# A four-layer hybrid diffusion step on one core: inputs requested at once, squares summed per token tile, layer norm in quarter slots with two forms of k-tile

## What is computed

```python
def rms_norm(x, g, eps=NORM_EPS):
    y = x * lax.rsqrt(jnp.mean(x * x, axis=-1, keepdims=True) + eps)
    return y * g
mod = jax.nn.silu(cond) @ w_mod[i] + b_mod[i]          # w_mod[i]: 1024 x 3072
shift, scale, gate = jnp.split(mod, 3, axis=-1)        # one set for context, one for latent tokens
h = rms_norm(x, norm_g[i]) * (1 + scale) + shift
x = x + gate * mixer(h @ w_in ...)
```

## Time and profile before

| | us |
|---|---|
| median of 3 runs | 2298.48 (2291.75 to 2299.92) |
| the profiled execution | 2295.94 |
| its span | 2294.1 |
| PE busy in the span | 2077.8 (91%) |
| DVE, ACT, POOL busy | 1179.2, 822.3, 550.6 |
| mean granted PE clock | 0.939 of full speed |

### The profile page before, as it was taken

One profiled execution on the slowest core, in us unless ns is written; L12 is line 12 of the kernel. 1 busy time (PEld: TensorE's weight loads), 2 busy tenths in 40 slices (PEclk: granted clock), 3 DMA queues, 4 the chain that ended last, 5 costly groups with the idle time before them and its releaser, 6 DMA issues.

```text
span 2294.1 us, 35050 instructions
## 1 busy us (share of the span) xinstructions
PE 2077.8 (91%) x14196; PEld 1773.8 (77%) x14196; DVE 1179.2 (51%) x2266; ACT 822.3 (36%) x1856; POOL 550.6 (24%) x440
## 2 busy tenths in 40 slices
PE   6899998889999998969979999998997979999888
PEld 3688886778988896959856868687876957888677
DVE  1577774564455554566544233251161666777544
ACT  3455564313444443041132232314121044565432
POOL 0422220343322420424310111102112532222112
PEclk9899998889999998979989999999998979999889
DMA  8221212322222222223313334324236221102001
GB/s 292 68 56 50 79 47 65 111 67 69 70 60 84 85 73 77 73 41 115 125 33 94 86 102 115 101 70 147 92 99 131 72 61 39 41 12 67 20 19 56
DMA packets 300622, 181.53 MB, mean 79 GB/s; under 512 B 59301, under 2 KB 276654, under 8 KB 300462
## 3 DMA queue, kind: packets, MB, share of 16 engines
q1 hardware_dynamic: 282894, 159.05, 23.6%
q10 hardware_dynamic: 17568, 20.24, 3.7%
HBM read 153.51 MB, written 25.74 MB: 78 GB/s over the span
## 4 chain that ended last, share of the span: by engine, by line
PE 73%; DVE 9%; ACT 9%; DMA 4%; issue 3%; SPq 1%; ACTq 1%; POOL 0%; DVEq 0%; POOLq 0%
PE pc L1673 19%; PE acc L1593 12%; PE acc L698 5%; PE acc L1765 4%; PE acc L1754 4%; PE acc L688 3%; PE pc L753 3%; PE pt L1776 3%; PE pt L698 2%; PE acc L1981 2%; PE acc L1993 2%; ACT ht L2178 2%; DMA out_mlstm_n<-amat 1%; PE acc L642 1%; ACT two L2227 1%
## 5 line engine op out<-in xcount | busy, mean ns | idle before, releaser
L1513 POOL TENSOR_TENSOR idle<-eps 128x1 f32<-128x1 f32 x144 | 41.9, 291 | 1677.8 <-PE pc L753 308.9
L1673 PE MATMUL pc<-hh,wh 128*128 128x320 f32 x1152 | 383.6, 333 | 34.0 <-DVE hl L2582 30.9
L1516 POOL TENSOR_TENSOR wl<-raw,wh 128x1024 fp32r<-128x1024 f32 x144 | 366.9, 2548 | 11.5
L1673 PE MATMUL pc<-hl,wh 128*128 128x320 f32 x1152 | 363.5, 316 | 0.0
L1673 PE MATMUL pc<-hh,wl 128*128 128x320 f32 x1152 | 363.4, 315 | 0.0
L1673 PEld LDWEIGHTS pc<-hh,wh 128*128 128x128 f32 x1152 | 223.1, 194 | 52.4 <-DVE hl L2582 27.1
L1673 PEld LDWEIGHTS pc<-hl,wh 128*128 128x128 f32 x1152 | 224.2, 195 | 0.2 <-issue 0.2
L1673 PEld LDWEIGHTS pc<-hh,wl 128*128 128x128 f32 x1152 | 223.2, 194 | 0.0
L2236 ACT COPY ht<-pt 128x512 f32<-128x512 f32 (+1 forms) x160 | 76.4, 525 | 214.3 <-PE pt L1776 214.2
L1514 POOL CAST wh<-raw 128x1024 fp32r<-128x1024 f32 x144 | 151.3, 1051 | 0.0
L1765 PE MATMUL acc<-ht,gvt 128*64 128x128 f32 x1344 | 100.5, 297 | 19.6 <-ACT ht L2241 15.2
(11 more groups left out here) (377 smaller groups left out, 4471.0 us busy)
## 6 DMA issues: line engine op xcount, KB each, us to landing
raw<-in_w_mod SPq DMA_DIRECT2D x144, 256.0 KB, 3.4
raw<-in_gqa_w_in SPq DMA_DIRECT2D x80, 256.0 KB, 3.4
raw<-in_diff_w_in SPq DMA_DIRECT2D x64, 256.0 KB, 3.8
raw<-in_mlstm_w_in SPq DMA_DIRECT2D x64, 256.0 KB, 3.4
praw<-in_w_mod SPq DMA_DIRECT2D x24, 512.0 KB, 9.5
raw<-in_gqa_w_out SPq DMA_DIRECT2D x32, 256.0 KB, 3.2
out_mlstm_C<-amat ACTq DMA_DIRECT2D x16, 512.0 KB, 8.0
raw<-in_mlstm_w_out SPq DMA_DIRECT2D x32, 256.0 KB, 3.2
```

The costliest lines, as they stand in the source:

```text
L1516: pool.tensor_tensor(wl[:, s], raw[:, r], wh[:, s].bitcast(F32), ALU.subtract).then_inc(w_full[s], 1)
L1673: ins = pe.matmul(pc[:, c:c + 320], w[:, sl, kt, :], h[:, kt, t:t + 320], start=kt == 0 and n == 0, stop=kt == KT - 1 and n == 2)
```

## The change

1. **Requests.** SP issues the constants' first part, all five x tiles (each into a place of its own in `whf` and `wlf`, the split weights' buffers), then 16 tiles of w_mod (thirds 0 and 1, 16 slots), the kv and q0 panels, then third 2 of w_mod (from tile 16 on behind `third_done` 1), then q1, z0 and the cache. The 20 small or late-needed DMAs (rows, lambda, sels, cs) are issued by ACT. POOL waits until x has been copied before its first split. `cache(0)` waits for two thirds and not three.
2. **Squares.** DVE squares each token tile as it arrives (128 x 1024) and adds over the eight k-tiles with a `tensor_reduce` whose innermost step is 128 elements; the result is a single 128 x 640 tile in `ht`, for which PE has 2 matmuls against ones. ACT no longer squares. The first tile is done before `cols` is copied, the other four after the lambda steps.
3. **Order of the prologue.** PE: x tiles 0 and 1, rows, x tiles 2 to 4, third 0, squares, third 1, turned 0, turned 1, kv unit, q0 half 0, third 2, q0 half 1, turned 2. ACT copies x tiles 0 and 1 before the silu of the conditioning and 2 to 4 behind the exponential. In layer 0 both reciprocals are taken before the modulation is formed.
4. **Norm of every layer.** `two` and `ht` are cut in four slots of 320 columns; DVE forms product kt and then rest kt-2. A k-tile is either plain (as before; kt 0 and 4 in the first half, kt 0, 2, 4, 6 in the second) or fused: DVE writes x·amul·rinv with a `scalar_tensor_tensor` (two in the first half), ACT adds the shift and rounds straight into `hh`, with no copy, and DVE forms `hl` = (u + shift) - hh with a `scalar_tensor_tensor` (two in the first half).

```diff
-PS = 17
+PS = 16
-        xtile = [two[:, :, 0:512], ht[:, :, 0:512]]
+        xtile = [whf[:, t, :] for t in range(3)] + [wlf[:, t, :] for t in range(2)]
+        XT = (0, 1, 1, 2, 2)
+        XN = (16, 32, 32, 32, 32)
+        PLAIN = (lambda kt: kt % 4 == 0, lambda kt: kt % 2 == 0)
+        def quarter(buf, j):
+            return buf[:, j % 4 // 2, 320 * (j % 2):320 * (j % 2) + 320]
...
@@ SP @@
+            sp.dma_start(consts[:, :, :], ...).then_inc(ident_in, 16)
+            for t in range(QT):
+                sp.dma_start(xtile[t], src).then_inc(xin_full[XT[t]], 16)
+            def thirds(u0, u1):
+                for u in range(u0, u1):
+                    if u == PS:
+                        sp.wait_ge(third_done, 1)
+                    sp.dma_start(praw[:, u % PS, :], A["w_mod"][0][...]).then_inc(praw_full[u // 4], 16)
+            thirds(0, 2 * KT)
...
-                    for what in FIRST:
+                    for k, what in enumerate(FIRST):
+                        if layer == 0 and k == 2:
+                            thirds(2 * KT, 3 * KT)
                         item(what, 0)
@@ POOL @@
+            pool.wait_ge(x_in, QT)
@@ PE, sum_squares @@
+                pe.wait_ge(*seen(sq_full))
+                for t, c in halves():
+                    pe.matmul(acc[b][:, c:c + 320], ones, ht[:, 0, t:t + 320], start=True, stop=True).then_inc(acc_full[b], 1)
@@ PE, gqa_layer @@
+                unit("q0", 0, 0)
+                if layer == 0:
+                    mod_third(2)
+                unit("q0", 0, 1)
                 if layer == 0:
                     mod_turned(2)
-                for half in range(2):
-                    unit("q0", 0, half)
@@ PE, layer 0 @@
+                    mod_third(0)
                     sum_squares()
                     seen.back(pe, ("acc", 0))
-                    mod_third(0)
                     mod_third(1)
                     mod_turned(0)
                     mod_turned(1)
-                    mod_third(2)
@@ ACT, modulate @@
+                        if PLAIN[half](kt):
+                            for a0, a1, g in parts:
+                                ins = act.activation(plain[:, a0:a1], u[:, a0:a1], ACT.Identity, bias=mod[:, kt, g:g + 1], scale=amul[:, kt, g:g + 1])
+                            ins.then_inc(xr_used, 1)
+                            act.wait_ge(*seen(xr_used))
+                            act.copy(high, plain).then_inc(ht_full, 1)
+                        else:
+                            for a0, a1, g in parts:
+                                ins = act.activation(high[:, a0:a1], u[:, a0:a1], ACT.Identity, bias=mod[:, kt, g:g + 1])
+                            ins.then_inc(ht_full, 1)
@@ DVE @@
+            def squared_tile(t):
+                dve.wait_ge(*seen(x_in))
+                sq = two.rearrange("p a c -> p (a c)")[:, 0:D].rearrange("p (k c) -> p k c", c=P)
+                step(dve.tensor_tensor(sq, x[:, :, t * P:(t + 1) * P], x[:, :, t * P:(t + 1) * P], ALU.mult))
+                ins = dve.tensor_reduce(ht[:, 0, t * P:(t + 1) * P], sq.rearrange("p k c -> p c k"), AX.X, ALU.add)
...
@@ DVE, normalise @@
+                def scaled(half, kt):
+                    if half or kt >= 4:
+                        dve.wait_ge(*seen(h_ready))
+                    if PLAIN[half](kt):
+                        ins = dve.tensor_tensor(u, x[:, kt, c0:c0 + 320], rinv[:, c0:c0 + 320], ALU.mult)
+                    else:
+                        for a0, a1, g in halved[half]:
+                            ins = dve.scalar_tensor_tensor(out=u[:, a0:a1], in0=x[...], scalar=amul[:, kt, g:g + 1], in1=rinv[...], op0=ALU.mult, op1=ALU.mult)
+                    ins.then_inc(xr_full, 1)
+                def low(half, kt):
+                    dve.wait_ge(*seen(ht_full))
+                    if PLAIN[half](kt):
+                        ins = dve.tensor_tensor(hl[:, kt, c0:c0 + 320], plain, high, ALU.subtract)
+                    else:
+                        for a0, a1, g in halved[half]:
+                            ins = dve.scalar_tensor_tensor(out=hl[...], in0=u[:, a0:a1], scalar=mod[:, kt, g:g + 1], in1=high[:, a0:a1], op0=ALU.add, op1=ALU.subtract)
+                    ins.then_inc(h_ready, 1)
+                for half in range(2):
+                    if half == 0 or modulated is None:
+                        dve.wait_ge(*seen(root_ready))
+                        step(dve.reciprocal(rinv[:, c0:c0 + 320], rinv[:, c0:c0 + 320]))
+                    if modulated is not None and half == 0:
+                        dve.wait_ge(*seen(root_ready))
+                        step(dve.reciprocal(rinv[:, 320:T], rinv[:, 320:T]))
+                        modulated()
+                    for kt in range(KT + 2):
+                        if kt < KT:
+                            scaled(half, kt)
+                        if kt >= 2:
+                            low(half, kt - 2)
```

More of the change, by code:

```diff
@@ L300, in build @@
         raw_full = [sem(f"raw_full{s}") for s in range(RAW)]
-        raw_used = [sem(f"raw_used{s}") for s in range(RAW)]
         w_full = [sem(f"w_full{s}") for s in range(SPL)]
@@ L305, in build @@
         acc_free = [sem(f"acc_free{b}") for b in range(2)]
-        xin_full = [sem(f"xin_full{b}") for b in range(2)]
+        xin_full = [sem(f"xin_full{b}") for b in range(3)]
+        ident_in = sem("ident_in")
         y_stored = [sem(f"y_stored{b}") for b in range(2)]
@@ L1424, in cache @@
                         if g == 0:
-                            sp.wait_ge(*((x_ready, sum(XR[:layer])) if layer else (third_done, 3)))
+                            sp.wait_ge(*((x_ready, sum(XR[:layer])) if layer else (third_done, 2)))
                         if g >= 2:
@@ L2138, in wide, with x_copied @@
                 return acc[b][0:rows, AO:AO + T]
+            turned = iter(range(QT))
+            def x_copied():
+                t = next(turned)
+                b, full = use()
+                act.wait_ge(*full)
+                act.copy(x[:, :, t * P:(t + 1) * P], acc[b][:, :].rearrange("p (k c) -> p k c", c=P)).then_inc(x_in, 1)
+            for dst, src in row_parts(rows, A):
+                act.dma_start(dst, src).then_inc(rows_in, 16)
+            c4 = A["consts"]
+            for i, n in enumerate(("q1", "k1", "q2", "k2")):
+                act.dma_start(lamr[0:1, i, :], A["diff_lambda_" + n]).then_inc(const_in, 16)
+            act.dma_start(sels[:, :], c4[:, 8 * P + 2 * NS:]).then_inc(const_in, 16)
+            act.dma_start(cs[:, :, :], c4[:, 4 * P:4 * P + 2 * NS].rearrange("p (a c) -> p a c", a=2)).then_inc(const_in, 16)
+            for t in range(2):
+                x_copied()
             act.wait_ge(eps_set, 1)
@@ L2146, in _ @@
             act.activation(lamt[0:1, 2:4], lamt[0:1, 0:2], ACT.Exp).then_inc(lam_step, 1)
-            for t in range(QT):
-                b, full = use()
-                act.wait_ge(*full)
-                act.copy(x[:, :, t * P:(t + 1) * P], acc[b][:, :].rearrange("p (k c) -> p k c", c=P)).then_inc(x_in, 1)
-            def norm_squares():
-                for kt in range(KT):
-                    if kt >= 2:
-                        act.wait_ge(*seen(sq_used))
-                    act.activation(two[:, kt % 2, :], x[:, kt, :], ACT.Square).then_inc(sq_full, 1)
-                seen(sq_used)
+            for t in range(2, QT):
+                x_copied()
             def roots():
@@ L2287, in y_high @@
                     act.copy(yh[:, b, :], gyt[:, b % 2, :]).then_inc(yhi_ready, 1)
-                for kind in ("kv", "q0"):
-                    for half in range(2):
-                        evac(kind, 0, half)
+                for kind, half in (("kv", 0), ("kv", 1), ("q0", 0), ("q0", 1)):
+                    evac(kind, 0, half)
+                    if layer == 0 and (kind, half) == ("q0", 0):
+                        third_copy(2)
                 k_root()
@@ L2533, in _ @@
                 use()
+            for t in range(1, QT):
+                squared_tile(t)
             def third_copy(r):
@@ L2594, in normalise @@
                         modulated()
-                    for kt in range(KT):
-                        if kt >= 2:
-                            dve.wait_ge(*seen(xr_used))
-                        dve.tensor_tensor(two[:, kt % 2, c0:c0 + 320], x[:, kt, c0:c0 + 320], rinv[:, c0:c0 + 320], ALU.mult).then_inc(xr_full, 1)
-                        if kt >= 1:
-                            rest(kt - 1, c0)
-                    seen(xr_used, 2)
-                    rest(KT - 1, c0)
+                    if half == 0:
+                        dve.wait_ge(*seen(mod_ready))
+                        dve.wait_ge(root_ready, seen.count[root_ready.name] + (modulated is None))
```

101 lines of the change are left out of this document (39 added, 62 removed).

## The result

| | median us | ratio to the kernel before | 95% |
|---|---|---|---|
| before (4 runs) | 2299.20 (2291.75 to 2310.69) | | |
| after (4 runs) | **2273.73** (2261.01 to 2279.36) | 0.989 | 0.9864 to 0.9916 |

The change makes the kernel 1.1% faster, 25.5 us by the medians; 2268 was forecast. The profiled execution took 2276.30, its span is 2274.5, the mean granted clock 0.943. In the last of the three sets of experiments one run of the kernel before took 2889.76 us at a mean granted clock of 0.667, and the ratios leave it out.

The account below looks back on a forecast made before the run. PE was taken to wait for `hl` in the norms and for late w_mod and serial squares in the prologue; gains of 16.7 (prologue) and 11.3 (norms), 28.0 from the profiled 2295.9, gave 2268 us, range 2254 to 2285.

Parts of the forecast that it names:

- likeliest case: Whole kernel: prologue and norm both gain as summed, 2268 us, own range 2260 to 2276, chance 0.58.
- Norm worth nothing: Rival, norm: a fused pair on DVE costs 0.96 us, only the prologue gains; 2285 us, chance 0.10.
- rows starve: Rival, prologue: small rows reach SBUF only at 35.8 us, `k_sums` 4.6 late; 2289 us, chance 0.07.
- R: Prologue: time at which the small rows are in SBUF, taken as 12 us, bounds 10.28 and 35.8.
- PE stays at the lower clock: Rival, units behind layer 0's kv unit: half units lose up to 3.7 us each; 2308 us, chance 0.03.
- The squares set the end: Rival, prologue: the reduce costs two to three times its elements, on the engines' chain; 2273 to 2278 us, chance 0.10.
- The norm: Norms of layers 1 to 3: DVE becomes the bound, stages shorten by 4.0, 2.7 and 4.6, together 11.3 us.
- The first product: Prologue, start of layer 0's norm: data and engine chains end together, first product at 39.6 us.
- By the data: Prologue: w_mod third 1 lands at 33.2, is multiplied and turned; first product at 39.3 us.
- the engines' chain: Prologue from the rows' arrival: transposes, silu, squares, sum, reciprocals, turning and modulation take 27.6 us, ending at 39.6.
- The squared tile: Prologue, DVE: product 1.2 and reduce 1.2 make 2.4 us a tile, four tiles 9.6.
- From there to `k_sums`: Layer 0: norm, POOL holds of 5.0, kv unit over at 62.3, then 14.0 to `k_sums` at 76.3, 16.7 us earlier.

Follow-up runs that it names:

- experiment 9: Changed kernel with POOL waiting so that its weight splits move out of the norm or beside the reciprocal: 2259.73 us, ratio 0.9862 to the kernel before.
- after again: The changed kernel with no edit, run once more in another job with a second profile: ratio 0.9902 to the kernel before.

## Why the prediction was right, step by step

2268 was forecast and 2273.73 measured, inside the range and inside the likeliest case's own; the gain was 25.5 us for a forecast of 28.0 from the profiled execution. No rival came true. *Norm worth nothing* fell (a pair of 0.59 to the next start), *rows starve* fell (R = 11.70, for 12), *PE stays at the lower clock* fell (q0's two halves took 7.1 us, less than the 8.49 of before). *The squares set the end* came true as a mechanism and not in its size: the reduce costs 1.6 times its elements and not two to three times, and all the squares 3.0 us for the 5 to 10 that they were priced at. The measured time also lies at the lower edge of its 2273 to 2278, but not by the squares alone, which are under half of what the first product was late.

**The norm: right.** Forecast 23.7, 24.5 and 20.1; measured 24.2, 23.9 and 20.0. The gain of 11.3 is the one measured, 3.5 + 3.2 + 4.6. That the sum fits to 0.1 us is luck in part, since layer 1 was 0.5 too short and layer 2 was 0.6 too long. Layer 3 came out term by term: its first product is held, 1.70 for 0.49, and the other 18.8 us stand beside the 18.9 of the prediction. DVE is the bound, as said.

**The first product: 6.6 us too early (39.6 for 46.2).** By the data 39.3 was a fair bound, but the engines' chain was mis-sized in three terms.
- The squared tile: 3.2 us and not 2.4, because the strided reduce takes 1.9 and not 1.2. The squares end at 33.9, 3.0 later than the 30.9 that my terms give.
- PE behind its wait: the sum took 2.47 where I had 0.9. PE had waited 8.36 us before it, and from 36 to 42 us the granted clock is 0.65 (the window below). Third 1 took 5.50 for 3.68. The prediction had PE at the full rate there and gave this no term.
- Third 1 is serial. I let it run beside the reciprocals and be ready before them; its 32 instructions end at 41.96, behind the second reciprocal's 40.4. Behind it I had counted one turning of 1.8, and both follow, 3.73.

```profile
36.00:42.00 6.00, 6.00 (x34) 1.42 (x34) 4.31 (x2) 0.56 (x2) 5.63 (x6) 0.65 1.02 352
```

**From there to `k_sums`: 4.0 us too long (36.7 for 32.7).** The holds were 2.9 and not 5.0 (the difference that experiment 9 makes), since kv and q0 are split from 36.21 on, beside the reciprocals and ahead of the norm, and only q1 meets a product. The kv unit is over 20.1 us after the first product (I had 22.7), and from there 12.6 us pass to `k_sums` (I had 14.0), because PE does all of q0 at the full rate: its matmuls go to full rate at 64.14, ahead of q0, and in the kernel before only at 87.4, inside it. Third 2 was not waited for, as costed, although SP asks for it only at 33.91 and not at about 24: four requests for the panels of kv and q0 held SP from 19.16 on for 14.71 us.

The two errors together turn 16.7 into 14.0. By its parts the prologue was not well forecast: up to the first product it was to gain 12.5 us and gained 5.9, and from there to `k_sums` it was to gain 4.1 and gained 8.1. So the forecast was right because the request order does what was said of it (taking it away costs 11.1 us) and because the norm's 11.3 were sized from rows, and it was near by luck as well, since an error of 4.0 made good most of one of 6.6.

## What to carry to other kernels

When a loop is moved from one engine to another, find out which engine is the bound *afterwards* and look again at who holds that engine: here the new bound was DVE, and POOL's splits, half hidden while ACT set the pace, became worth some 9 us that four waits brought back. Test the parts of a change together and apart: a step that costs nothing in one order (the second reciprocal) makes the first product 3.6 us later in another, 1.5 by itself and the rest by the lower clock that PE is granted behind its longer wait. And before a total that moves by less than half a per cent is explained, add up the stages of the trace: the stages repeated to 0.02 us where whole runs of one kernel differed by 16 to 18. A stage in which PE is at work behind a long wait is the exception: look there at how long the same instructions take in a second profile before its shift is put down to an edit.

## What the runs showed that I had not expected

PE's clock differs between executions of the very same program, far from anything that the change touches. Layer 0's attention in the two profiled executions of after: windows and PE of the first, then of the second, which by then is 1.6 us ahead.

```profile
126.00:130.00 4.00, 4.00 (x25) 2.49 (x25) 0.06 (x1) 1.28 (x4) 0.00 (x0) 0.50 0.00 0
```
```profile
124.13 1.25 PE L1812 MATMUL pt<-consts,gsq 128*128 128x2 f32 x10 [0.63 <-issue]
...
127.40 2.40 PE L1768 MATMUL acc<-ht,gvt 128*64 128x128 f32 x20
```
```profile
124.00:130.00 6.00, 6.00 (x51) 4.54 (x50) 2.86 (x7) 3.54 (x7) 0.00 (x0) 1.00 0.00 0
```
```profile
122.57 1.25 PE L1812 MATMUL pt<-consts,gsq 128*128 128x2 f32 x10 [0.65 <-issue]
...
124.96 1.31 PE L1768 MATMUL acc<-ht,gvt 128*64 128x128 f32 x20
```

PE waited 0.63 us in the one and 0.65 in the other, ahead of the same matmuls. In the first the granted clock then is 0.50, the lower of its two levels (1.2 GHz), with PE busy 4.00 of 4.00 us, and 20 matmuls take 2.40; in the second it stays at 1.00 and they take 1.31. `k_sums` starts within 0.02 us in both, and the first reciprocal of layer 1 is 3.2 us apart (489.49 and 486.31). Such losses come and go from run to run. They explain most of why the single pair of spans gives 19.6 us where the places give 25.3: from `k_sums` to the first reciprocal of layer 1, where the change touches nothing, before takes 406.0 us, after 410.5, and after again 407.3. What decides between the two I could not find; no run here separates it from chance.
